# Letting the planner of a Conformer step swap a product that it thinks has no free bank for the next one of the other kind

## The reference

```python
x = x + 0.5 * (silu(rms(x) @ w1_gate) * (rms(x) @ w1_up)) @ w1_down     # 1024 -> 2816 -> 1024
z = rms(x) @ w_in                                                       # 1024 -> 2500
A = differential_attention(z)     # 4 heads: softmax(q1 k1) - lam * softmax(q2 k2), times v of width 128
B = sparse_attention(z)           # 8 heads; an indexer of 4 heads keeps the best 256 keys of each query
x = x + concat(A, B) @ w_out
x = x + 0.5 * (silu(rms(x) @ w2_gate) * (rms(x) @ w2_up)) @ w2_down
```

## Time and profile before

| | |
|---|---|
| time, median of 3 | 2597.66 us (2597.21 to 2604.88) |
| the profiled execution, its own time | 2597.61 us |
| its span, first to last instruction | 2595.2 us |
| PE busy | 2503.7 us, 96% |
| DVE busy | 1447.8 us, 56% |
| ACT busy | 1033.3 us, 40% |
| PE's idle before the first matmul of a down product (L1400) | 23.0 us |

### The profile page before, as it was taken

The page is one execution under the profiler, slowest core; times in us unless marked ns, Lnnn a source line. Parts: engine busy times, 40 slices in busy tenths (PEclk is TensorE's granted clock), DMA queues, the critical chain, the costliest instruction groups (busy, mean ns, idle before and its releaser), DMA issues.

```text
span 2595.2 us, 36227 instructions
## 1 busy us (share of the span) xinstructions
PE 2503.7 (96%) x13547; PEld 2155.1 (83%) x13547; DVE 1447.8 (56%) x2884; ACT 1033.3 (40%) x1801; POOL 266.0 (10%) x363
## 2 busy tenths in 40 slices
PE   7999999999989999999999999999999999999998
PEld 5999999878867677778778889989888889888887
DVE  4534444454355358887655348888876545444444
ACT  3322222233332136566424337777565523222221
POOL 1100000014200001110014300000100001000000
PEclk7999999999999999999999999999999999999999
DMA  6212121233355253333433462232311132322221
GB/s 223 82 66 82 66 82 65 102 126 119 109 160 168 68 174 95 112 106 92 160 114 102 149 190 70 85 98 77 98 53 45 49 139 68 135 98 97 98 91 71
DMA packets 169004, 271.29 MB, mean 105 GB/s; under 512 B 72096, under 2 KB 104384, under 8 KB 168832
## 3 DMA queue, kind: packets, MB, share of 16 engines
q0 software_dynamic: 43200, 167.29, 19.2%
q1 hardware_dynamic: 125632, 101.69, 12.3%
HBM read 235.21 MB, written 35.29 MB: 104 GB/s over the span
## 4 chain that ended last, share of the span: by engine, by line
PE 81%; DVE 8%; issue 4%; ACT 3%; DMA 3%; SPq 1%; DVEq 0%; ACTq 0%; POOL 0%
PE bank L1383 12%; PE bank L1384 12%; PE bank L1385 12%; PE bank L1400 6%; PE bank L1401 6%; PE bank L1402 6%; PE bank L1420 4%; PE bank L1422 4%; PE bank L1421 4%; PE bank L1510 3%; DVE w_lo L1971 2%; PE bank L1479 1%; PE bank L1645 1%; PE bank L1493 1%; PE bank L1480 1%
## 5 line engine op out<-in xcount | busy, mean ns | idle before, releaser
L1971 DVE TENSOR_TENSOR w_lo<-raw,w_hi 128x1024 fp32r<-128x1024 f32 x320 | 385.9, 1217 | 148.5 <-ACT w_hi L1685 148.0
L1383 PE MATMUL bank<-XTh_a,w_hi 128*128 128x320 f32 x1408 | 441.4, 313 | 7.2 <-DVE w_lo L1971 2.9
L1385 PE MATMUL bank<-XTh_a,w_lo 128*128 128x320 f32 x1408 | 436.9, 310 | 0.0
L1384 PE MATMUL bank<-XTl_a,w_hi 128*128 128x320 f32 x1408 | 436.9, 310 | 0.0
L1685 ACT ACTIVATE w_hi<-raw 128x1024 fp32r<-128x1024 f32 x320 | 331.5, 1047 | 229.2 <-PE bank L1422 127.3
L1400 PE MATMUL bank<-w_hi,hid_hi 128*128 128x512 f32 x792 | 317.4, 401 | 23.0 <-DVE X_b L2002 8.2
L1401 PE MATMUL bank<-w_lo,hid_hi 128*128 128x512 f32 x792 | 313.1, 395 | 0.0
L1402 PE MATMUL bank<-w_hi,hid_lo 128*128 128x512 f32 x792 | 311.1, 393 | 0.0
L1383 PE MATMUL bank<-XTh_b,w_hi 128*128 128x512 f32 x704 | 284.1, 404 | 0.0
L1384 PE MATMUL bank<-XTl_b,w_hi 128*128 128x512 f32 x704 | 279.0, 396 | 0.0
L1385 PE MATMUL bank<-XTh_b,w_lo 128*128 128x512 f32 x704 | 278.9, 396 | 0.0
(11 more groups left out here) (318 smaller groups left out, 4053.7 us busy)
## 6 DMA issues: line engine op xcount, KB each, us to landing
raw<-in_w_gate POOLq DMA_DIRECT2D x44, 1024.0 KB, 5.7
raw<-in_w_up POOLq DMA_DIRECT2D x44, 1024.0 KB, 5.7
raw<-in_w_down POOLq DMA_DIRECT2D x44, 1024.0 KB, 5.3
raw<-in_w_in POOLq DMA_DIRECT2D x16, 1024.0 KB, 5.4
s_k_in<-in_cache_diff_k SPq DMA_DIRECT2D x16, 512.0 KB, 3.8
s_v_in<-in_cache_diff_v SPq DMA_DIRECT2D x8, 1024.0 KB, 5.6
raw<-in_w_out POOLq DMA_DIRECT2D x8, 1024.0 KB, 5.4
q_rows_b<-q_scr SPq DMA_DIRECT2D x80, 64.0 KB, 2.1
```

The lines of the kernel that those rows point to most:

```text
L1383: pe.matmul(out, hi[:, k], XTh[g][:, k, lo:up], start=(k == 0), stop=False)
L1384: pe.matmul(out, hi[:, k], XTl[g][:, k, lo:up], start=False, stop=False)
L1385: last = pe.matmul(out, low[:, k], XTh[g][:, k, lo:up], start=False, stop=(k == KD - 1))
L1971: dve.tensor_tensor(hilo(w_lo, u)[:, :, 0:width_of(u)], raw_part(u), hilo(w_hi, u)[:, :, 0:width_of(u)].bitcast(F32), ALU.subtract).then_i ...
```

## The change

Before a main item is taken, the new class `Main` asks the estimate whether that item could start: for a down product when its bank is free, for the first part of a gate/up product when its bank is free (`Lists.start`). If the estimate says more than 0.2 us later than PE, it looks at up to seven items ahead for the first one of the other kind, and takes that one first if the estimate lets it start at least 0.2 us earlier and `may_pass` holds: the last part of an up product may not be moved, a weight unit may not be begun ahead of another one that is not begun, and it may not be finished ahead of an older one that isn't. The rest of `merge` is as before, apart from the form of `owed`. No instruction is added or removed; the work is the same, in another order.

```diff
--- before.py
+++ after.py
@@ -456,6 +456,11 @@
         if item[0] in self.HOLDS:
             self.free[self.held.pop((self.HOLDS[item[0]],) + item[1:])] = t
 
+    def start(self, item):
+        if item[0] == "gu":
+            return max(self.at["PE"], self.gu[0] if item[5] == 0 else 0.0)
+        return max(self.at["PE"], self.downs[0])
+
     def main(self, item):
         kind = item[0]
         if kind in ("gu", "down", "mm"):
@@ -494,17 +499,66 @@
                 self.book("DVE", t, 1.5)
 
 
+class Main:
+
+
+    REACH = 8
+
+    def __init__(self, items, first):
+        self.items = list(items)
+        self.number, self.left = {}, {}
+        for m in self.items:
+            if m[0] in ("gu", "down", "mm"):
+                u = unit_of(m)
+                self.number.setdefault(u, len(self.number))
+                self.left[u] = self.left.get(u, 0) + 1
+        self.started = set()
+        self.items = self.items[first:]
+        for m in items[:first]:
+            self.took(m)
+
+    def took(self, m):
+        if m[0] in ("gu", "down", "mm"):
+            self.started.add(unit_of(m))
+            self.left[unit_of(m)] -= 1
+
+    def may_pass(self, m, passed):
+        u = unit_of(m)
+        if m[0] == "gu" and m[2] and m[5] + K_PART[PAIRS[m[1]][1]] == KD:
+            return False
+        if u not in self.started and any(unit_of(x) not in self.started for x in passed):
+            return False
+        return self.left[u] > 1 or not any(self.left[v] for v, n in self.number.items() if n < self.number[u])
+
+    def take(self, lists):
+        n = 0
+        if self.items[0][0] in ("gu", "down") and lists.start(self.items[0]) > lists.at["PE"] + 0.2:
+            for k in range(1, min(self.REACH, len(self.items))):
+                m = self.items[k]
+                if m[0] not in ("gu", "down"):
+                    break
+                if m[0] != self.items[0][0]:
+                    if lists.start(m) < lists.start(self.items[0]) - 0.2 and self.may_pass(m, self.items[:k]):
+                        n = k
+                    break
+        m = self.items.pop(n)
+        self.took(m)
+        return m
+
+
 def merge(main, side, first=0, spare=10.0):
 
-    owed = {m for k, m in enumerate(main) if any(x[0] == "late" for x in main[k + 1:k + 3]) and m[0] != "late"}
     for tenth in range(40):
         lists = Lists(0.1 * tenth)
         out, n, left = list(main[:first]), 0, 0.0
-        for m in main[first:]:
+        rest = Main(main, first)
+        while rest.items:
+            m = rest.take(lists)
             out.append(m)
             lists.main(m)
             left += 1.4 if n == len(side) and m[0] in ("gu", "down", "mm") else 0.0
-            while n < len(side) and m not in owed and lists.can_follow(side[n]):
+            owed = m[0] != "late" and any(x[0] == "late" for x in rest.items[:2])
+            while n < len(side) and not owed and lists.can_follow(side[n]):
                 lists.side(side[n])
                 out.append(side[n])
                 n += 1
```

## The result

The changed kernel takes 2625.0 us (median of 4 runs, 2621.05 to 2628.31) where the kernel before took 2598.5 in the same session: ratio 1.0096, 95% interval 1.0075 to 1.0118. It is 1% slower, and slower than the predicted range (2591 to 2619). The profiled execution took 2621.05 us, with a span of 2618.5, which is 23.3 more than before; the other three took 2624.68 to 2628.31, with a mean granted clock of 0.979 to 0.983 where it had 0.991.

What follows compares the result with a forecast made beforehand. PE, busy 96% of the span, was taken as the bound. Terms -8.4 - 1.7 - 1.5 + 9.3 + 6.0 + 1.0 + 3.5 = +8.2 on 2597.6 gave 2605.8 us, range 2591 to 2619.

Steps and rivals of the forecast that it cites:

- three quarters of the bank waits: Both differential stretches: three quarters of PE's 11.2 us waiting for down products' banks would go, -8.4 us in all.
- the clock given back: Differential stretch of group B, around the longest bank wait (2.8 us): full clock level regained, -1.7 us.
- waits that stay: Rival: the chip waits at other down products, 11.6 us of gains vanish, losses stay; 2617.4 us, chance 0.07.
- Differential A: Differential stretch of group A: besides fewer bank waits, denser filling, 123 products instead of 105, -1.5 us.
- Sparse A: Sparse blocks 21 to 35 of group A run without products between, 0.9 us idle a block: +9.3 us.
- Indexer of B: Group B's blocks 36 to 41 run without a product, 1.0 us idle a block: +6.0 us.
- The clock: In the sparse stretch of A and indexer of B: two clock falls, half hidden in waits, +3.5 us.
- The rivals that ended at 2616 and 2617: Clock falls repeatedly in the two lonely stretches: 2616, chance 0.15; down products wait elsewhere, gains vanish: 2617.4, chance 0.07.
- The rest: Three products fewer in blocks 60 to 75, a few less ahead of block 36: +1.0 us.

Runs made afterwards that it cites:

- the kernel with the products moved: The kernel before with its own order and give, FFN products between blocks 21 and 35 and 36 and 42 put behind the last block: 2625.6 us, ratio 1.0089.

## Why the prediction was wrong

**The mechanism was right as far as it went.** The estimate lost its gaps, `merge` had to take a wider `give`, and blocks ran alone. The two runs that are the change's halves show it: in both differential stretches the swap gains at each `give` (differential A -8.2, -18.4, -11.8 at the old values, 1.4, 1.6; differential B -3.9, -6.0, -17.6), and a `give` of 1.6 costs, with the swap and without. By the median times over before's:

```
give          old      1.4      1.6
no swap     1.0000   1.0063   1.0220
swap        1.0077   0.9965   1.0096
```

At the old values the swap loses all the same, by the items that its list leaves over.

**The step that failed** is the pricing of the wider `give` at the sparse stretch of A and the indexer of B alone. In differential B my terms (three quarters of the bank waits, and the clock given back) made -7.6; measured is +4.4, 12 of the 15.1 us by which the sum (+8.2 against +23.3) was short. The waits for the two banks went even more fully than assumed (9.3 of 11.2 us, as far as a bank is named). But the `give` of 1.6 alone made this stretch 22.0 us longer, and the swap took back 17.6. The prediction had waits that stay as a rival, but no wait that is new there: 6.2 us at the gate/up bank and 4.6 at the attention's `ex_b`.

**Differential A.** Terms of -2.6 and -1.5 against -9.7: under-sized, in the direction foretold. PE's idle time is 5.6 us of it, and the granted clock went from 0.99 to 1.00.

**Sparse A.** +9.3 against +13.3. The idle time was hit: from block 20 to the end of block 35 it is 13.4 us, against 4.2 before. Up to the first scores of block 35, where the table's stretch ends, it is 12.1 against 3.4, so 4.6 of the 13.3 us are not idle time. The traces tell where most of that is. A turning or weighing matmul that another follows at once counts some 0.1 us, to the start of the next; the last one ahead of idle time counts 0.27 to 0.28 in full. In the changed kernel PE goes idle 30 times in this stretch, before 11 times: 19 x 0.17 = 3.2 us, an estimate from the starts and ends in the two traces. The sum counted a wait by its idle time alone.

**Indexer of B.** +6.0 against +8.4: 6.8 us of idle time, with `q_lo_b` ahead of the scores as foretold, 1.1 us a block and not 1.0; the other 1.6 us are not idle time, which I did not take apart.

**The clock.** +3.5 for two falls, half hidden. In the changed kernel it stayed at 1.00 all through the lonely sparse blocks and fell right behind them. Windows of PE:

```profile
1235.00:1240.00 5.00, 3.75 (x25) 1.00 0.08 25
1240.00:1245.00 5.00, 3.72 (x24) 0.84 0.06 16
1245.00:1250.00 5.00, 5.00 (x20) 0.50 0.06 16
...
1260.00:1265.00 5.00, 2.14 (x13) 0.89 0.77 312
1265.00:1270.00 5.00, 5.00 (x22) 0.77 0.63 209
```

That is 5 x (0.16 + 0.50 + 0.11 + 0.23) = 5.0 us of full level, where before lost 1.7 from block 35 to 36; the second fall stands beside a wait of 2.9 us for the output rows. So the size was about right and the place wrong. The rule of the Trainium skill that I weighed ("TensorE: Matmul & The Clock Gate", section "A second HAM failure mode: psum-queue depth-cycling", which tells of a kernel whose clock swings by short idle spots) did not hold inside this stretch, with 11.7 us idle in 52.4; in the kernel with the products moved, like blocks at other times did show it (0.50 and 0.67). The rivals that ended at 2616 and 2617 are nearer to the time, but not by their reasons: the clock did not fall again and again, and the waits for the down products' banks did go.

**The rest.** +1.0 against 2.8 in sparse B and +0.7 beyond the clock's 5.0 from block 35 to 36.

**What stays open.** From block 35 to 36, kernels with one and the same order until shortly ahead of block 36 differ: before and the swap in the second merge alone 32.1 and 36.4, the two with the swap at 1.4 in the table 33.1 and 39.5. A cost of 5 us there is within what that stretch does by itself, so the +5.7 is not shown to come from the lonely blocks. Why the differential stretches swing by 10 us between a `give` of 1.4 and 1.5 I did not find out; so the 22.0 us of differential B belong to the list made at 1.6, and are no price of `give` in general.

## What to carry to other kernels

Where a planner searches a parameter until a condition holds, a change to its costs acts twice: by the new order, and by where the search now stops. Measure the two apart, with the parameter held, before judging either; here a rule that gains in two stretches lost to the search that it upset, and holding `give` at 1.4 made a gain of 0.35 to 0.4% of a loss of 1%. With the swap in both merges, the old values, 1.4, 1.5 and 1.6 gave 1.0077, 0.9965, 1.0033 and 1.0096, so the gain is that of one list among four and not shown to be that of the rule. And price the new parameter in every stretch that it orders, not only in those where the order looks strange.

## What the runs showed of the hardware

The granted clock is not a function of the order alone. Two kernels with the same order until shortly ahead of block 36 (the swap at 1.4 in both merges, and in the first alone), windows of PE behind block 35, which begins at 1265.0 in the first and at 1262.8 in the second. The first kernel:

```profile
1265.00:1270.00 5.00, 3.92 (x23) 1.00 0.04 13
1270.00:1275.00 5.00, 4.84 (x27) 0.65 0.04 13
1275.00:1280.00 5.00, 5.00 (x18) 0.67 0.14 28
```

and the second, which has two more falls soon after (one in the last two rows, one from 1300 to 1310 with 0.80 and 0.86):

```profile
1265.00:1270.00 5.00, 3.75 (x25) 0.88 0.00 0
1270.00:1275.00 5.00, 5.00 (x22) 0.50 0.04 13
1275.00:1280.00 5.00, 5.00 (x15) 0.59 0.42 128
1285.00:1290.00 5.00, 2.65 (x11) 0.93 1.01 412
1290.00:1295.00 5.00, 5.00 (x26) 0.73 0.31 95
```

In the first of these windows PE was idle for 1.1 and 1.25 us; the same 1.25 us at 1235 of the changed kernel left the clock at 1.00. I can't say from these rows which idle spot lets it fall.
